# Mix attention of a six-layer network: probability maps and all query and key sets turned by VectorE squares and a way through DRAM instead of by TensorE transposes

## The reference, cut to what matters

```python
h = rms_norm(x, mix_norm[l])
aq, ak, av, bq, bk, bv, cq, ck, cv, cg, gates = jnp.split(h @ w_in[l], split_points, axis=-1)   # 7680 columns
qa, ka = rope(_rms_f32(aq, ...)), rope(_rms_f32(ak, ...))      # 4 heads x 2 maps x 64
y_a = diff_attention(qa, ka, va, lam, lam_init, a_subln[l])    # softmax(map 0) - lam * softmax(map 1), times v
y_b = chunk_attention(qb, kb, vb, b_rel_bias[l])               # 8 heads x 64, relative bias, softmax, times v
y_c = retention(qc, kc, vc, cg, c_out_norm[l])                 # 4 heads x 64, a fixed decay and no softmax
merged = g0 * (y_a @ w_branch_a[l]) + g1 * (y_b @ w_branch_b[l]) + g2 * (y_c @ w_branch_c[l])
x = x + merged @ w_out[l]
```

## Time and profile before

| what | value |
|---|---|
| three timed runs, us | 1820.05, 1818.6, 1818.33 (median 1818.6) |
| span of the profiled execution, us | 1816.7 |
| TensorE busy | 1797.5 us, 99% |
| POOL busy | 1365.0 us, 75% |
| DVE / ACT busy | 942.8 us / 905.1 us |
| DMA | 366.61 MB, mean 202 GB/s |
| granted TensorE clock, mean | 0.999 of full speed |

### The profile page before, as it was taken

The page is one execution under the profiler, slowest core; times in us unless marked ns, Lnnn a source line. Parts: engine busy times, 40 slices in busy tenths (PEclk is TensorE's granted clock), DMA queues, the critical chain, the costliest instruction groups (busy, mean ns, idle before and its releaser), DMA issues.

```text
span 1816.7 us, 25068 instructions
## 1 busy us (share of the span) xinstructions
PE 1797.5 (99%) x9322; PEld 1482.3 (82%) x9322; DVE 942.8 (52%) x1756; ACT 905.1 (50%) x1337; POOL 1365.0 (75%) x568
## 2 busy tenths in 40 slices
PE   6999999999999999999999999999999999999999
PEld 5888888887889888887888888888888878888887
DVE  4673766678655524776553230714095865143152
ACT  3334424764456644455554644464445565545442
POOL 2624544559868898987689798969897858888885
PEclk9999999999999999999999999999999999999999
DMA  9853885748775775565466566567655645656653
GB/s 366 299 201 93 278 301 164 196 157 301 245 279 188 221 216 194 172 209 165 132 187 195 175 195 195 193 184 232 195 195 181 186 139 163 194 160 211 190 194 128
DMA packets 200697, 366.61 MB, mean 202 GB/s; under 512 B 32868, under 2 KB 54356, under 8 KB 200020
## 3 DMA queue, kind: packets, MB, share of 16 engines
q1 hardware_dynamic: 197568, 357.39, 61.6%
q10 hardware_dynamic: 3028, 7.86, 1.1%
HBM read 364.12 MB, written 6.13 MB: 204 GB/s over the span
## 4 chain that ended last, share of the span: by engine, by line
PE 98%; DMA 0%; ACTq 0%; ACT 0%; DVE 0%; POOL 0%; issue 0%; DVEq 0%
PE ps L1258 26%; PE ps L1260 26%; PE ps L1259 26%; PE ps L1384 3%; PE ps L1385 3%; PE ps L1386 3%; PE ps L1949 1%; PE ps L1951 1%; PE ps L1950 1%; PE ps L1306 1%; PE ps L1876 1%; PE ps L1655 1%; PE ps L1626 1%; PE ps L1636 1%; PE ps L1516 1%; PE ps L1921 1%
## 5 line engine op out<-in xcount | busy, mean ns | idle before, releaser
L616 POOL TENSOR_TENSOR w_lo<-raw,w_hi 128x1024 fp32r<-128x1024 f32 x556 | 1346.0, 2458 | 403.4 <-ACT w_hi L654 382.2
L1258 PE MATMUL ps<-w_hi,act_rows_r 128*128 128x512 f32 x2064 | 814.8, 395 | 3.2 <-POOL w_lo L616 3.1
L1260 PE MATMUL ps<-w_hi,act_rows_r 128*128 128x512 f32 x2064 | 804.8, 390 | 0.0
L1259 PE MATMUL ps<-w_lo,act_rows_r 128*128 128x512 f32 x2064 | 804.5, 390 | 0.0
L654 ACT ACTIVATE w_hi<-raw 128x1024 fp32r<-128x1024 f32 x556 | 571.1, 1058 | 359.4 <-DMA raw<-in_ffn_w_up 96.5
L1258 PEld LDWEIGHTS ps<-w_hi,act_rows_r 128*128 128x128 f32 x2064 | 387.9, 188 | 89.9 <-issue 8.6
L1260 PEld LDWEIGHTS ps<-w_hi,act_rows_r 128*128 128x128 f32 x2064 | 387.8, 188 | 81.8
L1259 PEld LDWEIGHTS ps<-w_lo,act_rows_r 128*128 128x128 f32 x2064 | 388.1, 188 | 77.2
L2604 DVE STREAM_TRANSPOSE ps<-proj 32x256 f32<-32x256 f32 (+1 forms) x384 | 166.6, 434 | 6.5
L2585 DVE TENSOR_TENSOR proj<-proj,ps 128x1024 f32<-128x1024 f32 (+1 forms) x18 | 20.4, 1132 | 252.2 <-PE ps L1260 247.8
L1384 PE MATMUL ps<-act_rows_r,w_hi 128*128 128x512 f32 (+1 forms) x288 | 101.4, 352 | 0.0
(11 more groups left out here) (245 smaller groups left out, 1559.9 us busy)
## 6 DMA issues: line engine op xcount, KB each, us to landing
raw<-in_w_in SPq DMA_DIRECT2D x120, 512.0 KB, 3.8
raw<-in_ffn_w_gate SPq DMA_DIRECT2D x88, 512.0 KB, 4.3
raw<-in_ffn_w_up SPq DMA_DIRECT2D x88, 512.0 KB, 4.3
raw<-in_ffn_w_down SPq DMA_DIRECT2D x88, 512.0 KB, 3.4
proj<-in_ada_w SPq DMA_DIRECT2D x39, 512.0 KB, 7.8
pt<-in_ada_w SPq DMA_DIRECT2D x38, 512.0 KB, 6.4
raw<-in_pool_w_in SPq DMA_DIRECT2D x32, 512.0 KB, 7.4
raw<-in_na_w_in SPq DMA_DIRECT2D x32, 512.0 KB, 5.4
```

The lines of the kernel that those rows point to most:

```text
L616: pool.tensor_tensor(w_lo[:, s, :], raw[:, s, :], w_hi[:, s, :].bitcast(F32), ALU.subtract).then_inc(lo_done, 1)
L1258: pe.matmul(o, h, hi, start=start, stop=False)
L1259: pe.matmul(o, h, lo, start=False, stop=False)
L1260: return pe.matmul(o, c, hi, start=False, stop=stop)
```

## The change

Every transpose on TensorE in the mix stage is dropped. DVE turns 32x32 squares within their 128 partitions (all four rows of squares in one instruction) into a staging area. SP writes this to a scratch tensor in DRAM by one DMA. Four more DMAs read it back, each to 32 partitions, so that the squares change places. The five sets are keys A, queries A, keys B, queries B and C (its queries and keys together); the maps are those of units 0 to 7.

The last number of a set in `MIX_SETS` is a group: the write of the set is in SP's list 8 groups after it and the four reads one group later still. In the list of SP `keep_map(i)` stands behind the send of group 25 + 2i and `place_map(i)` behind the send of group 26 + 2i. On both lists a set goes ahead of a map. On TensorE `values(i)` moves to odd G = 21 + 2i for A and to G = 22 + 2i for B, behind `scores(i+3)`. It writes bank 6 for both. DVE's `combined(i)` moves to G = 22 + 2i for A and G = 24 + 2i for B, each behind the logits of that G. Queries and maps of A are now read from SBUF by a stationary pattern with 8 and 3 elements from one column to the next. Keys of A and B and maps of B are read in runs of 32, keys of C with 8 elements from one to the next.

```diff
-MIX_TURN_AT = {13: (2, 3), 19: (6, 7), 31: (8, 9)}
+MIX_SETS = ((AK, 4, 7), (AQ, 0, 10), (BK, 12, 13), (BQ, 8, 18), (CQ, 16, 29))
...
+        def mix_out_bank(i):
+            return 6 if i < MIX_SOFT else 7
+        def map_block(i, m):
+            n = map_blocks(i)                      # 3 for A, 6 for B
+            return map_turned(i, [[n, P]], m) if i < 4 else map_turned(i, [[32 * n, 4], [1, 32]], 32 * m)
+        def still_heads(chunk, rows, t):
+            base = chunk // 4 * 4
+            return free(qt[rows, base, 0:1], [[8, P]], 2 * (chunk - base) + t)
+        def moving_heads(chunk, rows, t, n):
+            base = chunk // 4 * 4
+            return free(qt[rows, base, 0:1], [[32, n], [256, 4], [1, 32]], 32 * (2 * (chunk - base) + t))
...
SP
+            def keep_map(l, i):
+                sp.wait_ge(dve_done, dve_s.count(("am_t", l, i)))
...
+                sp.dma_start(map_rows[i % 2, :, 0:n], map_squares(i, [[1, n]])).then_inc(maps_kept[i % 2], 16)
+            def place_map(l, i):
+                sp.wait_ge(maps_kept[i % 2], 16 * (MIX_SOFT // 2 * l + i // 2 + 1))
...
+                for kq in range(4):
+                    src = bass.AP(map_rows.tensor, i % 2 * P * 768 + n * kq, [[768, 32], [32 * 768, 4], [1, n]])
+                    sp.dma_start(map_turned(i, [[n, 4], [1, n]], 0, slice(32 * kq, 32 * kq + 32)), src).then_inc(maps_in[i % 2], 16)
...
+                        if layer is not None:
+                            for q, (_, _, at) in enumerate(MIX_SETS):
+                                if g == at + SLOTS:
+                                    keep_set(layer, q)
+                                if g == at + SLOTS + 1:
+                                    place_set(layer, q)
+                        i = (g - MIX_FIRST - SLOTS - 1) // 2
+                        if layer is not None and 0 <= i < MIX_SOFT:
+                            (keep_map if g % 2 else place_map)(layer, i)
...
TensorE
-                    if even and 2 <= i < MIX_UNITS + 2:
+                    if even and 4 <= i - 3 < MIX_SOFT:
+                        values(i - 3)
+                    if even and MIX_SOFT <= i - 2 < MIX_UNITS:
                         values(i - 2)
-                    if not even and 1 <= i <= MIX_SOFT:
-                        probabilities(i - 1)
-                    for k in MIX_TURN_AT.get(G, ()):
-                        turn_heads(k)
+                    if not even and 0 <= i - 2 < 4:
+                        values(i - 2)
...
ACT
+                    if G % 2 == 1 and 4 <= i - 3 < MIX_SOFT:
+                        b_high(i - 3)
...
DVE
+                def set_squared(q):
+                    if len(MIX_SETS) * l + q:
+                        dve.wait_ge(sets_kept, 16 * (len(MIX_SETS) * l + q))
+                    for t in range(NT):
+                        rows = free(proj[:, 0:1], [[P, 4], [32, 4], [1, 32]], MIX_SETS[q][0] + t * IN_COLS)
+                        if q in (SET_AK, SET_BK):
+                            last = dve.transpose(set_blocks([[64, 4], [256, 4], [1, 32]], 32 * t), rows)
+                        else:
+                            last = dve.transpose(set_blocks([[2, 4], [256, 4], [8, 32]], t), rows)
...
                             logits(i)
-                        if i >= 2:
+                        if 3 <= i < 7:
+                            combined(i - 3)
+                        if 4 <= i - 4 < MIX_SOFT:
+                            combined(i - 4)
+                        if i >= MIX_SOFT + 2:
                             combined(i - 2)
                         if i < MIX_SOFT:
                             maxima(i)
...
+                            dve.wait_ge(dve_done, dve_s.count(("rows", l, 2)))
+                            set_squared(SET_C)             # G == 28
...
+                    if G == 23:
+                        queries_scaled()                   # queries B, 128x1024, after they have landed
                     if i < 4:
                         maps_joined(i)
                     elif 4 <= i < MIX_SOFT:
                         rows_scaled(i)
+                    if i < MIX_SOFT:
+                        squares_of_map(i)                  # one transpose of 128x384 (A) or 128x768 (B)
```

More of the change, by code:

```diff
@@ L230, in program @@
         decay_in = sem("decay_in")
+        sets_kept, sets_in = sem("sets_kept"), [sem("sets_in0"), sem("sets_in1")]
+        maps_kept, maps_in = ([sem(f"{n}{k}") for k in range(2)] for n in ("maps_kept", "maps_in"))
         out_done = sem("out_done")
@@ L590, in _ @@
                 ffn_weights(I["ffn1_w_gate_2"][l], I["ffn1_w_up_2"][l], I["ffn1_w_down_2"][l], tables=True)
[L591 removed]
+                narrow(I["w_in_2"][l], 15, 512, f"mix_in{l}", order=MIX_ORDER, layer=l)
                 for j in range(6):
@@ L1042, in root @@
                     c = MIX_STAT[n]
+                    if n == 1:
+                        act.activation(rstat[:, c:c + 16], stat[:, c:c + 16], ACT.Sqrt,
+                                       bias=eps_64[:]).then_inc(act_done, act_s.one(("hrms", l, n)))
+                        return
                     act.activation(rstat[:, c:c + 16], stat[:, c:c + 16], ACT.Sqrt, bias=eps[:],
                                    scale=1.0 / HD).then_inc(act_done, act_s.one(("hrms", l, n)))
[L1046 to L1051, removed]
                 def evicted(n, how):
@@ L1113, in mix @@
                     if G == 20:
-                        act.wait_ge(dve_done, dve_s.count(("keys", l, BK)))
+                        act.wait_ge(dve_done, dve_s.count(("set", l, SET_BK)))
                         for h in range(4):
@@ L1846, in group @@
                     last.then_inc(group_used, 1)
[L1848 to L1855, removed]
-                def scores(i):
[L1859 to L1863, removed]
+                def scores(i):
+                    for q in {0: (SET_AK, SET_AQ), 4: (SET_BK,), 8: (SET_C,)}.get(i, ()):
+                        set_landed(pe, l, q)
+                    if i == 4:
+                        pe.wait_ge(dve_done, dve_s.count(("bq", l)))
                     read_out(4)
@@ L1867, in scores @@
                         q, keys = (i, 4 + i) if i < 4 else (4 + i, 8 + i)
-                        parts = ((0, slice(0, P), slice(0, P)), (SEQ, slice(P, SEQ), slice(0, SEQ)))
+                        parts = ((0, 0, 0, 1), (SEQ, 1, 0, 2))
                     else:
                         q, keys = 10 + i, 8 + i
-                        parts = ((0, slice(0, P), slice(0, SEQ)), (SEQ, slice(P, SEQ), slice(P, SEQ)))
-                    for o, still, moving in parts:
+                        parts = ((0, 0, 0, 2), (SEQ, 1, 1, 1))
+                    heads = moving_heads if i < MIX_SOFT else moving_between
+                    for o, still, first, n in parts:
                         for c in range(2):
                             rows = slice(c * HD, (c + 1) * HD)
-                            n = moving.stop - moving.start
-                            last = pe.matmul(ps[:, 4 + c, o:o + n], qt[rows, q, still], qt[rows, keys, moving], start=True, stop=True)
+                            last = pe.matmul(ps[:, 4 + c, o:o + n * P], still_heads(q, rows, still), heads(keys, rows, first, n),
+                                             start=True, stop=True)
                     last.then_inc(pe_done, pe_s.one(("as", l, i)))
                     held[4] = held[5] = (dve_s, ("al", l, i))
-                def probabilities(i):
-                    pe.wait_ge(dve_done, dve_s.count(("aj", l, i)))
-                    for c in range(1 if i < 4 else 2):
-                        read_out(6 + c)
-                        for k in range(3):
-                            last = pe.transpose(ps[:, 6 + c, k * P:(k + 1) * P], mix_rows_of(i, [[1, P]], c, k * P), ident[:])
-                        last.then_inc(pe_done, pe_s.one(("at", l, i, c)))
-                        held[6 + c] = ((dve_s if c else act_s), (f"apt{c}", l, i))
                 def values(i):
@@ L2712, in mix @@
                 dve.tensor_tensor(k, k, head_rstd(0), ALU.mult).then_inc(dve_done, dve_s.one(("rows", l, 0)))
+                dve.wait_ge(dve_done, dve_s.count(("rows", l, 0)))
+                set_squared(SET_AK)
                 dve.wait_ge(act_done, act_s.count(("hsq", l, 1)))
@@ L2718, in mix @@
                 inverse(1)
-                dve.wait_ge(dve_done, dve_s.count(("rows", l, 0)))
-                keys_turned(AK, 4)
+                dve.wait_ge(dve_done, dve_s.count(("rows", l, 1)))
+                set_squared(SET_AQ)
                 squares(2)
```

128 lines of the change are left out of this document (71 added, 57 removed).

## The result

The changed kernel takes **1852.9 us** (median of 4 runs, 1850.6 to 1855.3) against 1818.5: ratio 1.0186, interval 1.0172 to 1.0200, so 34 us slower. The forecast was 1820.4, with a range to 1836. The profiled execution of after is the slowest of its four and has a span of 1853.5 us, that of before 1816.7, so there are 36.8 us to explain.

A forecast was written before the change was run, and what follows sets the result against it. TensorE, busy 99% of the span, was taken as the bound. Span 1816.7 - 13.2 (transposes) + 15.0 (pauses, 7.5 us a layer) = 1818.5, plus 1.9 around it: 1820.4 us. Own range 1815 to 1827; 8 in 10, 1808 to 1836.

The forecast's parts named there:

- the price of the transposes (-13.2 us): Mix stage, TensorE: 60 transposes a layer go, 0.11 us each, 6.6 us a layer, 13.2 us in two.
- I take 0: TensorE's loads of queries and maps of A with steps of 8 and 3 elements were costed at no extra time.
- the bound of 22.9: Upper bound for strided loads at half rate: 104 loads a layer, 0.11 us more each, 22.9 us in two layers.
- I take 6.1: Pause of TensorE at G = 32, for bank 6's read-out and set C's landing: 6.1 us a layer.
- G = 34, 1.4 us: TensorE pauses 1.4 us a layer while DVE does logits and `combined` after scores(9).
- The trips hold: DRAM trips of 7.6 to 11.4 us: the likeliest fits A's lead of 9.3 us or a little under.
- Before G = 16 DVE is relieved, so the first scores are not late: DVE has less work before G = 16, so the first scores were given no delay.
- Rival 3: Trips through DRAM too long: TensorE waits at `values(0)` to `values(3)`, 2 us in each of 8 units, about 1830; chance 0.15.
- Rival 4: Granted clock falls to 0.5 for a group after each pause, 2.75 us twice: 1826; counted within the forecast's upper range.
- SP holds weights at no cost: Sends of weights queue behind SP's wait for a map, up to about 5 us at G = 29 to 31; costed at nothing.
- DVE's 128x768 near 1.0 us: Sign to look for: DVE transposes of 128x768, a map of B, estimated at 0.99 us.
- 0.72 us for 512 elements: Estimated time of one DVE transpose of half a set, 512 elements per row.

The follow-up runs named there:

- the kernel without them: Changed kernel with values of units 0 to 3 one group later, banks 7 and 6 in turn, scores of units 8 and 9 reading set B: 1819.1 us, 1.0005.

## Why the prediction was wrong, point by point

Four steps of the sum failed: strided reads taken at 0, the lead of `values(0)`, the length of the pause at G = 32, and the granted clock, which the sum left out.

- *What bounds, and the price of the transposes (-13.2 us):* right. The ledger has -6.6 a layer, and without pauses the gain comes out less the strides' price.
- *"I take 0" for strided reads:* wrong, and called the weakest choice. Measured 0.05 us a load on the path (the load itself takes 324 ns instead of 186), with step 3 as with step 8, plus 0.8 us a unit for C's scores: 3.2 + 1.2 + 1.6 = 6.0 us a layer, 12 in two, about half of the bound of 22.9. Most of C's part lies with the moving operand, also read with step 8: packing the loads alone took only 0.1 of the 0.8. The prediction named no price for moving operands. Its reason for the 0, that runs of 32 cost TensorE what whole rows do, stood in no row of before; it came true (keys in runs of 32, with packed loads, are at 1.04 us for 1.05) but says nothing of a step of 8.
- *G = 32, "I take 6.1":* the mechanism right, the size not: 9.05 us of idle time (7.50 + 1.55), +12.3 by the ledger. Counted from the start of scores(6) (873.60), map 6 was done after 14.0 us for 12.7 (set C's two transposes took 2.14 for 1.4), and set C landed after 22.3 for 18.7 to 20.3: 1.3 us of this excess come from map 6 and 1.1 from the last landing, 5.3 us and not up to 4.2, while SP's issues took 0.5 less. The scaling of unit 6 was the slow one again, 3.18 us, and for that case the prediction's own figures were 6.3 to 7.9; 6.1 lies below them.
- *G = 34, 1.4 us:* 1.54, right, and the half clock behind it was not counted.
- *"The trips hold", values A at a lead of 9.3 us:* wrong for `values(0)`. The store of map 0 was issued at 833.9 and the last read landed at 843.2: a trip of 9.3 us, inside the predicted 7.6 to 11.4, with the set of B's queries issued between its store and its reads. It was the lead that failed: TensorE was there at 840.6, 6.7 us after the store, because the map was late. "Before G = 16 DVE is relieved, so the first scores are not late" is the sentence that broke, at the staging area's store. Stored at 830.3, a trip of the same length would have landed about 1 us before TensorE came; this is an estimate, as no run changes the staging area alone. TensorE was idle for 2.71 and 2.39 us in the two layers, +5.5 in the first. `values(1)` to `values(3)` did not wait, but for `values(1)` that was luck: its map's trip took 10.3 us, and the pause before had held TensorE back. With that pause shorter it waits for 1.65 us (set of B's queries one group later). Rival 3 had this mechanism for eight units.
- *Rival 4, "2.75 us twice":* it belonged into the forecast. The steps were at half clock behind three pauses in the first layer and two in the second, and for up to ten steps of 0.20 us extra.
- *SP holds weights at no cost; DVE's 128x768 near 1.0 us:* both right (0.978). Of the estimates for DVE's transposes, 0.72 us for 512 elements was right for the keys (0.690) and wrong for writes with step 8 (1.157).

By steps, the first layer was off by 18.8 us (19.7 against 0.9): strides 6.0, `values(0)` 5.2 with its stride left out, G = 32 5.4 and G = 34 1.9 beyond their strides, 18.5 in all. No single term would have brought the forecast to 1836; what failed is that costs with a shown risk were each set at their low end, and the clock left out of every one. That the pauses with the clock were the loss is shown by the kernel without them. That the clock fell because of them is shown by their absence only; what sets its fall is not, and one pause of 3.61 us passed without it.

## What to carry to other kernels

Where an engine is at 99%, let a new producer on a longer way land well ahead of its reader, and look for what makes the producer itself late, here a staging area with one place and a collision with GpSimd. With the maps' trips one group longer, banks in turn, unit 6 scaled by ScalarE and the sets' trips left out, the change is 5 us faster than before, where it had been 34 slower; what each of these four is worth there by itself no run shows. Before moving work off it, price how the moved data will be read (step of a load, step of a moving operand), since 60 transposes at 0.11 us, 6.6 us a layer, were nearly given back by 88 strided loads at 0.05 and by C's scores, whose loads and moving operand are both strided, 6.0 us together. And where two waits lie over each other, take both away before judging either.

## What the hardware did that I had not expected

- A strided stationary load: 324 ns at step 8 against 186 to 199 packed (64 rows), 260 at step 3 against 190 packed (128 rows); a DVE transpose of 128x512 took 1157 ns writing with step 8 and 690 in runs of 32.
- The steps of TensorE fell to half clock behind idle times from 2.11 us up (2.39, 2.71, 3.66, 4.69, 6.7 to 8.0 us), but not at once everywhere, and in one case, 3.61 us, not at all. They stayed whole behind 1.03, 1.65, 1.78 and 1.84 us. Behind 1.54 or 1.55 us at G = 34, after the fall at G = 32, they fell again in five cases, the first layer of the changed kernel among them, and did not in three, its second layer among them.
- DVE's four scalings took 1.01 us alone, 3.1 beside one subtraction of GpSimd, 5.05 beside two, and moving them to ScalarE was worth 11.3 us in one kernel and nothing in another.
